# Row items' down projection: 256 moving weight columns per matmul in place of 512

## The reference

```python
hg = lax.ragged_dot(xs, w_gate_e, sizes)
hu = lax.ragged_dot(xs, w_up_e, sizes)
ys = lax.ragged_dot(jax.nn.silu(hg) * hu, w_down_e, sizes)   # 3584 -> 1024: the down projection
ys = ys * gates.reshape(-1)[order][:, None].astype(ys.dtype)
out = jnp.zeros_like(xt).at[tok].add(ys)
```

## Time and profile before

| what | value |
|---|---|
| device time, median of three runs | 3547.31 us |
| span of the profiled execution, first to last instruction | 3546.6 us |
| matmuls in the program's run, and weight loads | 25975 and 25975 |
| matmul busy time (modelled ends) | 3492.9 us |
| VectorE, ScalarE, GpSimd busy | 1898.8, 1573.3, 198.7 us |
| row items' down projection | 1680 matmuls of 512 columns in ten stretches, 2538.6 to 3529.5 us |

### The profile page before, as it was taken

One profiled execution on the slowest core, in us unless ns is written; L12 is line 12 of the kernel. 1 busy time (PEld: TensorE's weight loads), 2 busy tenths in 40 slices (PEclk: granted clock), 3 DMA queues, 4 the chain that ended last, 5 costly groups with the idle time before them and its releaser, 6 DMA issues. The chain is left out here.

```text
span 3546.6 us, 69579 instructions
## 1 busy us (share of the span) xinstructions
PE 3492.9 (98%) x25975; PEld 3294.5 (93%) x25975; DVE 1898.8 (54%) x2868; ACT 1573.3 (44%) x2305; POOL 198.7 (6%) x214
## 2 busy tenths in 40 slices
PE   9999899999999999999999999999999999999998
PEld 8888799999999989889999999999999888898886
DVE  6455543333333555364445445446555577686774
ACT  4455433333333343354344444435454465554654
POOL 1000000000000000021101001001000010010100
PEclk9999999999999999999999999999999999999999
DMA  5111333333333322265546446446566575665754
GB/s 201 35 47 46 137 96 95 98 94 120 98 96 96 125 94 90 84 211 155 185 157 204 166 161 203 164 157 232 194 209 216 188 241 196 200 233 190 228 196 163
DMA packets 157624, 540.74 MB, mean 152 GB/s; under 512 B 23608, under 2 KB 23616, under 8 KB 157504
## 3 DMA queue, kind: packets, MB, share of 16 engines
q1 hardware_dynamic: 129584, 467.74, 40.3%
q0 software_dynamic: 24464, 65.04, 5.3%
q10 hardware_dynamic: 3456, 6.29, 0.5%
HBM read 515.54 MB, written 45.45 MB: 158 GB/s over the span
## 5 line engine op out<-in xcount | busy, mean ns | idle before, releaser
L311 DVE TENSOR_TENSOR wl<-wraw,wh 128x1024 fp32r<-128x1024 f32 x884 | 1082.2, 1225 | 1148.6 <-ACT wh L307 1148.0
L307 ACT ACTIVATE wh<-wraw 128x1024 fp32r<-128x1024 f32 x884 | 933.8, 1057 | 1081.4 <-PE ps L325 1020.7
L325 PE MATMUL ps<-ex,wh 128*128 128x256 f32 (+2 forms) x4484 | 851.2, 289 | 2.2 <-issue 1.9
L325 PE MATMUL ps<-xs,wh 128*128 128x256 f32 x5248 | 824.4, 279 | 4.3 <-DVE qAl L821 1.9
L325 PEld LDWEIGHTS ps<-xs,wh 128*128 128x128 f32 x5248 | 699.8, 189 | 15.9 <-issue 9.9
L325 PEld LDWEIGHTS ps<-ex,wh 128*128 128x128 f32 x4484 | 704.5, 188 | 3.0 <-issue 2.9
L325 PE MATMUL ps<-ex,wl 128*128 128x288 f32 (+2 forms) x2240 | 647.2, 289 | 0.0
L325 PE MATMUL ps<-xs,wl 128*128 128x256 f32 x2624 | 514.5, 278 | 0.0
L2003 PE MATMUL ps<-ex,wh 128*128 128x480 f32 x1344 | 445.2, 382 | 0.0
L325 PEld LDWEIGHTS ps<-ex,wl 128*128 128x128 f32 x2240 | 420.8, 188 | 0.0
L325 PEld LDWEIGHTS ps<-xs,wl 128*128 128x128 f32 x2624 | 398.3, 189 | 0.0
(11 more groups left out here) (339 smaller groups left out, 3931.8 us busy)
## 6 DMA issues: line engine op xcount, KB each, us to landing
wraw<-in_w_expert SPq DMA_DIRECT2D x676, 512.0 KB, 3.3
wraw<-in_w_main SPq DMA_DIRECT2D x208, 512.0 KB, 3.6
hT<-in_xT POOLq DMA_DIRECT2D x2, 2048.0 KB, 9.5
h_d<-hT POOLq DMA_DIRECT2D x2, 2048.0 KB, 10.5
hT<-h_d POOLq DMA_DIRECT2D x2, 2048.0 KB, 13.0
xrow_d<-rows ACTq DMA_DIRECT2D x16, 256.0 KB, 2.6
yraw<-y_d POOLq DMA_DIRECT2D x4, 768.0 KB, 7.9
tabA_d<-extA_d POOLq DMA_DIRECT2D x1, 2560.0 KB, 13.6
```

Of the source, the lines that this page charges most:

```text
L307: act.activation(wh[:, j], wraw[:, j], ACT.Copy).then_inc(hi_done, 1)
L311: dve.tensor_tensor(wl[:, j], wraw[:, j], wh[:, j].bitcast(F32), ALU.subtract).then_inc(lo_done, 1)
L325: mm = pe.matmul(out[:, s], a, b[:, s], start=first and part == 0 and c == 0, stop=last and part == 2 and d == n)
```

## The change

`down_rows_pe` calls `product` without `wide=True`. The condition in `product` then gives w = 256, and each term of 512 columns is issued as two matmuls of 256 columns, with the same stationary operand, into the two halves of the same PSUM bank. No other call, wait or transfer is changed.

```diff
@@ down_rows_pe
                         ch, cl = (a[:, 2 * u + ff, P * tb:P * tb + P] for a in (mah, mal))
                         w = slice(512 * ff, 512 * ff + 512)
                         mm = product(pe, bank(b + tb), ch, cl, wh[:, j, w], wl[:, j, w],
-                                     first and ff == 0, last and ff == 1, wide=True)
+                                     first and ff == 0, last and ff == 1)
                 mm.then_inc(unit_used, 1)
```

## The result

The changed kernel takes 3567.76 us in the median of 5 runs (3564.95 to 3571.64). The kernel before, timed beside it in 5 runs, stays at 3547.31 (3545.86 to 3551.17). The ratio is 1.006, 95% interval 1.0049 to 1.0071. The forecast was 3543.8 with a range from 3541.8 to 3556; the measured time lies 11.8 us above its upper end, and it is slower where no change clear of the spread was forecast.

What follows compares the result with a forecast made beforehand. TensorE was taken as the bound, the edited down projection's time being the sum of start-to-start matmul pitches. In the quick pace -3.7 us plus 0.2 for entries gave -3.5 us, 3543.8 us, range 3541.8 to 3556.

Steps and rivals of the forecast that it cites:

- Instructions: TensorE's written-out row bodies: 672 more matmuls and loads each, fetched as some tens of packets; 0, at most +1 us.
- what would prove me wrong: Changed profile: a third pitch, TensorE idle in written-out stretches from late instructions, or TensorE waiting for `wl`.
- Which pace?: Down projection's 256-column streams: all taken as quick, 113.4 ns not 117.8, -3.7 us; quick everywhere given 0.46.
- rival 3: Down projection: slow after transposes and in first stretches of 240-token items; +8.1 us, 3555.4, chance 0.09.
- The 0.2 us for the entries: Stream restarts after `xg` transposes: ten entries at 0.02 us more than now, +0.2 us.
- The uneven cut as what lifts a stream: Down projection has no uneven cut, so a slow stream would stay slow to its stretch's end; no size of its own.
- Weight load per matmul, hidden: Down projection: 1680 more loads of 0.19 us, each beside the preceding matmul's streaming, already included in 113.4 ns.
- Rival 4: Down projection: a fixed price per matmul that quick rows hide, 10.4 ns more per term; +17.5 us, 3564.8, chance 0.03.
- rival 5: Down projection: small fixed price, pitch between the paces at 115.6 ns; +3.7 us, 3551.0, chance 0.04.
- The Trainium skill's fixed price: Each warm matmul costs its columns at 2.4 GHz plus 2.5 ns; +4.2 us for 1680 terms, ending at 3551.5.
- Waits and converters: Down projection's weight feed: no wait added or removed, ScalarE's and VectorE's 1.06 and 1.23 us fit inside a unit; no cost.
- The tail: From the last matmul's start to the kernel's end nothing is touched; distance unchanged at 17.1 us.

Runs made afterwards that it cites:

- second_long: Kernel before with only the down projection's second halves cut to 256 columns and more gate and up turns written out (bodies 1896 and 1772); 3572.58 us, ratio 1.0073.
- tail512: Changed kernel with the last three units of each second stretch kept at 512 columns, ahead of the loop's turn; 3556.55 us, ratio 1.0031.
- entry512: Changed kernel with 512 columns kept in each stretch's first unit and the unit behind the second transposes, 256 ahead of the turn; 3554.8 us, one run.
- limit: Changed kernel with eight (256 tokens) or one (240 tokens) first-stretch units kept at 512 columns, bodies 1640 and 1676; 3566.73 us, one run.
- uneven: Changed kernel with one product near each start, and again behind the second transposes, cut unevenly at column 320; 3569.94 us, ratio 1.0065.
- uneven_other: Changed kernel with the same products cut unevenly at column 192 (256-token items) or 384 (240-token items); 3575.04 us, one run.
- split_first: Kernel before with only the first half of each item's down projection cut to 256 columns; 3549.75 us, ratio 1.0009.

## Why the prediction was wrong, step by step

- **"Instructions", "so 0, with up to +1 us": this step failed, and it is worth +10.8 us** (7.5 of three stops, 3.3 of half clock behind two of them; `second_long`, `tail512`, `entry512` and `limit` give the condition). I took the instruction queue as a matter of bandwidth, "some tens of packets more", and the number was right: 32 more. What matters is when a packet comes. The question that I didn't ask of the earlier trace rows was *when* the 84 packets move: a window on the last two items would have shown none at all. The loop ran from what TensorE holds, and 672 more instructions in a body of 1160 could end this. I looked for idle time in the stretches and not at the turn between items. None of the six rivals has this mechanism, though "instructions arriving late" stood in the list of what would prove me wrong.
- **"Which pace?", quick for all: wrong, and the rivals had it right.** What came is rival 3 but for one first stretch: 1176 terms slow and 504 quick give 1176 x 6.6 - 504 x 2.2 = +6.7 us, and the trace shows +1.1 + 5.6 = +6.7. Both pitches (113.4 and 117.8 ns) and their prices came true to the tenth. I had weighed one entry after transposes that became quick against one that didn't and took the kind one; all five were slow. The reason given for it was wrong as well: the start that followed a stop of TensorE is the one at 2385.8, while the one after `vbT` transposes, the lasting slow one, had no idle time ahead of it. The 0.2 us for the entries don't show: the unit between the transposes costs 0.08 us more in each item, which is what 12 x 6.6 ns give.
- **The uneven cut as what lifts a stream**: contradicted by `uneven` and `uneven_other`.
- **Weight load per matmul, hidden:** right. 1120 loads for 1120 matmuls in each group, and 113.4 ns with a load in each where the stream is quick. Rival 4's 10.4 ns and rival 5's middle pitch appear nowhere. The Trainium skill's fixed price ("TensorE: Matmul & The Clock Gate", section "Wait — 56ns, not 53.3ns?") would be +4.2 us; no stretch shows it, the quick ones have a difference of the other sign.
- **Waits and converters:** right. ScalarE's idle time still ends on the matmuls, and no matmul inside a stretch waits for `wl`.
- **The tail:** right, 17.1 us. That what TensorE gains or loses, the end gains or loses: right, 18.97 of 19.2 us.
- **The gate and up of the next item, taken as untouched:** wrong by about 1.1 us in item 3 and by the 3.3 us of half clock. The edit changes how these streams begin.

With the pace as it came and no stops the time would have been 3547.3 + 6.7 = 3554.0, or 3555.2 with the gate and up of item 3, inside the range; the stops carry it out.

Open is what puts a stream into its pace. In the windows read, the down projection's streams right behind transposes are slow and those behind 512 columns are quick in second stretches, but the first stretches of the 240-token items are slow in most kernels (`split_first`, `tail512`, `entry512`, two of three in the changed one) and quick in the third of the changed kernel and in `limit` (267 matmuls in 30 us from 3005 on, 113.4 ns). In item 3 `limit` and `entry512` have the same matmuls there, behind a gate and up of the same length (149.4 us), and still one is quick and the other slow, so the matmuls just ahead don't decide it alone.

No row names what takes the 4.4 ns per matmul. Why some refilled turns fetch a second late packet is open as well.

## What to carry over

Before an edit makes a written-out loop body longer, count its instructions on that engine and look at whether its instruction queue moves packets at all while the loop turns; a queue that is silent there means that the body is held, and the price of outgrowing that is a stop at each turn, not bandwidth, unless long matmuls stand ahead of the turn. Splitting matmuls has two prices, the pitch and the instructions, and short matmuls ahead of the turn leave a late fetch uncovered. Where a trace shows two paces for one shape, price both for each entry of the stream, and take the worse one unless the same entry is seen to be quick.

## What the hardware showed

- TensorE's loop ran from held instructions up to a body of 1640 and fetched itself again from 1676 on, at 9 packets of 16 KB per turn.
- A refilled turn costs 2.1 to 3.2 us of idle TensorE behind 256-column matmuls (3.19 once, in `uneven_other`; four times with a second stop of 1.8 to 2.3), and 0.07 to 0.11 us behind 512-column ones. The Trainium skill ("Runtime: NRT & Kernel Launch", section "Instruction fetch mechanics") calls the crossing of a block's boundary mostly hidden; that agrees with the straight parts of these bodies, and at a loop's turn only with the kernels with 512 columns ahead of it.
- In the changed kernel, behind two of the stops the granted clock was 0.50 and 0.58 for some 3 us, behind a third, as long, it was 1.00.
- The trace puts such a stop down to "issue" or to whichever semaphore came last, here `wl`, whose converter was itself waiting for TensorE.
- A stream of fp32r matmuls of one shape has two lasting pitches at one granted clock: 113.4 and 117.8 ns at 256 columns, 165.4 and 166.7 for 480 and 240 in turn.
